# Two orders of the solved 16x16 blocks through DRAM, and no first transpose for four of the five tiles

## The reference, cut to what matters

```
a_mat = where(strict, einsum('nbhik,nbhjk->nbhij', kb, kc) * decay, 0.0)
t_inv = triangular_solve(eye + a_mat, eye, lower=True)
u = t_inv @ (vc * beta);  w = t_inv @ (kb * exp(gc))
def step(S, ...):
    v_new = u_i - w_i @ S
    o = (q_i * exp(g_i)) @ S + intra @ v_new
    S = S * exp(g_last) + (k_i * exp(g_last - g_i)).T @ v_new
```

## Time and profile before

| | us |
|---|---|
| median of the runs | 1290.6 |
| the profiled execution | 1286.11 |
| its span | 1284.3 |
| PE busy | 1144.1 (89%) |
| DVE busy | 445.2 (35%) |
| ACT busy | 329.5 (26%) |
| GpSimd (POOL) busy | 180.2 (14%) |

### The profile page before, as it was taken

One profiled execution on the slowest core, in us unless ns is written; L12 is line 12 of the kernel. 1 busy time (PEld: TensorE's weight loads), 2 busy tenths in 40 slices (PEclk: granted clock), 3 DMA queues, 4 the chain that ended last, 5 costly groups with the idle time before them and its releaser, 6 DMA issues.

```text
span 1284.3 us, 15885 instructions
## 1 busy us (share of the span) xinstructions
PE 1144.1 (89%) x6262; PEld 611.6 (48%) x6262; DVE 445.2 (35%) x843; ACT 329.5 (26%) x587; POOL 180.2 (14%) x295
## 2 busy tenths in 40 slices
PE   2699999999998987889999999999649999999990
PEld 1244456666664666888444444444333333333320
DVE  1223035877764542555420300214431111111115
ACT  4012134454453533332321000111202111111111
POOL 0000020011000257571100000000110111111100
PEclk9799999999989999899999999999959999999995
DMA  8801243343302110210231111150616999999936
GB/s 325 360 9 66 90 141 114 132 148 141 122 1 77 47 29 22 87 26 1 94 131 66 51 35 46 66 196 33 245 43 241 385 392 377 375 391 380 385 112 249
DMA packets 44063, 199.98 MB, mean 156 GB/s; under 512 B 18320, under 2 KB 23904, under 8 KB 31952
## 3 DMA queue, kind: packets, MB, share of 16 engines
q1 hardware_dynamic: 28256, 142.03, 28.8%
q10 hardware_dynamic: 4608, 30.18, 6.2%
q0 software_dynamic: 11120, 26.70, 5.8%
HBM read 190.69 MB, written 22.87 MB: 166 GB/s over the span
## 4 chain that ended last, share of the span: by engine, by line
PE 76%; DVE 9%; DMA 6%; POOL 3%; issue 3%; ACT 3%; SPq 0%; DVEq 0%; POOLq 0%; ACTq 0%
PE bank L1649 24%; PE bank L2195 11%; PE bank L1753 8%; PE bank L2216 6%; DMA arena<-h_scratch,arena 3%; PE bank L2052 3%; PE bank L2050 3%; PE bank L1802 2%; PE bank L2183 2%; PE bank L1739 2%; PE bank L1607 2%; PE bank L1908 1%; PE bank L1710 1%; DMA arena<-in_w_blocks 1%; DVE arena L1287 1%
## 5 line engine op out<-in xcount | busy, mean ns | idle before, releaser
L1649 PE MATMUL bank<-arena 128*128 128x512 f32 x720 | 315.9, 595 | 4.4 <-DVE arena L1113 3.5
L1649 PEld LDWEIGHTS bank<-arena 128*128 128x128 f32 x720 | 135.3, 190 | 169.4 <-issue 168.3
L2195 PE MATMUL bank<-arena 128*32 128x512 f32 x1536 | 172.2, 599 | 1.3 <-DVE arena L1562 1.3
L1753 PE MATMUL bank<-arena 128*128 128x320 f32 x384 | 122.0, 452 | 0.5 <-ACT arena L822 0.5
L2195 PEld LDWEIGHTS bank<-arena 128*32 128x32 f32 x1536 | 48.2, 110 | 107.8 <-issue 107.8
L2216 PE MATMUL bank<-arena 128*32 128x512 f32 x768 | 87.4, 595 | 0.8 <-ACT arena L1053 0.8
L1753 PEld LDWEIGHTS bank<-arena 128*128 128x128 f32 x384 | 68.6, 194 | 26.4 <-issue 2.1
L1575 DVE TENSOR_TENSOR arena<-arena,bank 128x256 f32<-128x256 f32 x24 | 10.1, 421 | 175.6 <-ACT arena L1047 175.6
L710 POOL DMA_INDIRECT y_scratch<-arena x24 | 24.3, 1013 | 247.8 <-DVE arena L1568 219.7
L1440 DVE TENSOR_TENSOR arena<-arena,bank 128x512 f32<-128x512 f32 x10 | 6.9, 689 | 135.8 <-PE bank L2052 135.8
L976 ACT ACTIVATE arena<-bank 128x512 f32<-128x512 f32 x20 | 11.9, 597 | 151.5 <-PE bank L1649 151.4
(11 more groups left out here) (298 smaller groups left out, 1517.4 us busy)
## 6 DMA issues: line engine op xcount, KB each, us to landing
arena<-in_w_up SPq DMA_DIRECT2D x32, 2048.0 KB, 10.1
arena<-in_w_blocks SPq DMA_DIRECT2D x27, 2048.0 KB, 7.9
arena<-in_w_down ACTq DMA_DIRECT2D x28, 1024.0 KB, 8.6
arena<-y_scratch SPq DMA_DIRECT2D x10, 512.0 KB, 7.5
arena<-in_bias POOLq DMA_DIRECT2D x3, 1536.0 KB, 11.6
arena<-in_w_down SPq DMA_DIRECT2D x4, 1024.0 KB, 8.0
arena<-in_x SPq DMA_DIRECT2D x5, 512.0 KB, 9.1
gram_scratch<-arena SPq DMA_DIRECT2D x10, 256.0 KB, 2.4
```

Of the source, the lines that this page charges most:

```text
L1649: last = mm(bank, hT[:, k, tok0[i]:tok0[i] + P], w[:, k, :], start=(k == 0), stop=(k == KC - 1))
L1753: last = mm(banks[5 + half][:, 0:HTOK], w[:, k, :], hT[:, k, half * HTOK:(half + 1) * HTOK], start=(k == 0), stop=(k == KC - 1))
L2195: last = mm(banks[2 + e % 2][at, :], rowsT[e % 2][:, k, at], eup[expert % SLOTS_W][:, k, :], start=(k == 0), stop=(k == KC - 1))
```

## The change

SP writes the solved blocks twice, once as they are and once with each 16x16 block transposed, and reads both back. For the second, GpSimd makes a transposed copy of the 64 blocks at the end of `solve`. GpSimd spreads out four matrices where it spread out two: `invT` and `inv` of both directions. For tiles 1 to 4 PE's first transposes and ACT's first copies go, and `couple(p, 1)` waits for the spread instead. Tile 0 stays as it was. The diff, cut to its core:

```diff
 def solved_out(p):
     sp.dma_start(t["solve_scratch"][p], src[0:64].rearrange("p c i -> p (c i)"))...
+    if p:
+        sp.dma_start(t["turned_scratch"][p], solve_raw[0:64].rearrange("p i c -> p (i c)")).then_inc(S["solve_io"], 16)
 def solved_back(p):
     sp.dma_start(solved_in if p else first_in, rows_of("solve_scratch"))...
+    if p:
+        sp.dma_start(turned_in, rows_of("turned_scratch")).then_inc(S["solve_back"], 16)
 def spread_out(p):
-    pool.wait_ge(S["solve_back"], 16 * p)
-    for d in range(2):
-        if d == 0 and p >= 2: pool.wait_ge(S["step_mm0"], step_at(p - 2, "vn"))
-        if d == 1 and p >= 1: pool.wait_ge(S["x_mm1"], NL * p)
-        dst = U["invT"][p % 2] if d == 0 else U["inv"]
+    pool.wait_ge(S["solve_back"], 32 * p)
+    for kind in ("invT", "inv"):
+        for d in range(2):
+            if kind == "invT" and p >= 2: pool.wait_ge(S[f"step_mm{d}"], step_at(p - 2, "vn"))
+            if kind == "inv": pool.wait_ge(S[f"x_mm{d}"], NL * p)
+            dst = U["invT"][p % 2] if kind == "invT" else U["inv"]
+            src = solved_in if (kind == "invT") == (d == 0) else turned_in
             step(pool.tensor_tensor(dst..., src..., blk..., ALU.mult), "spread")
 def solve(p, first, last):
-        step(pool.tensor_tensor(below, below, part, ALU.subtract), "solved" if n == 1 else "pool_step")
+        step(pool.tensor_tensor(below, below, part, ALU.subtract))
+    if last == SUB - 1:
+        step(pool.tensor_copy(solve_raw[0:64].rearrange("p i c -> p c i"), solve_x[0:64]), "solved")
 # ACT, per tile
-    inv_out(p, 1)
+    if p == 0: inv_out(p, 1)
 # PE
 def couple(p, n):
-        pe.wait_ge(S[f"inv{d}"], NL * p + n)
+        if p and n == 1:
+            pe.wait_ge(S["spread"], 4 * (p - 1) + 3 + d)
+            pe.wait_ge(S[f"xs{d}"], NL * p)
+        else:
+            pe.wait_ge(S[f"inv{d}"], turn_at(p, n))
...
-                if p + 1 < T:
-                    turn_inv(p + 1, 1)
```

More of the change, by code:

```diff
@@ L233, in build @@
         first_in = first_t[:, 0:2 * H_B * SUB].rearrange("p (u i) -> p u i", u=2 * H_B)
-        solved_in = solve_t[:, 0:2 * H_B * SUB].rearrange("p (u i) -> p u i", u=2 * H_B)
+        solved_in, turned_in = (solve_t[:, o:o + 2 * H_B * SUB].rearrange("p (u i) -> p u i", u=2 * H_B) for o in (0, 2 * H_B * SUB))
         assert solve_at + 2 * SUB * SUB <= KC * HALF
@@ L424, in solve_at_io, with turn_at @@
         def solve_at_io(p, k):
-            return 48 * (p - 1) + {"blocks": 32, "solved": 48}[k]
+            return 64 * (p - 1) + {"blocks": 32, "solved": 64}[k]
+        def turn_at(p, n):
+            return NL * p + n if p == 0 else NL + (NL - 1) * (p - 1) + n - 1
         def step_at(p, k):
@@ L485, in solved_back, with rows_of @@
                     sp.wait_ge(S["first_io"], 48)
-                back = bass.AP(t["solve_scratch"].tensor, p * 64 * SUB * SUB, [[SUB, P], [P * SUB, 2 * H_B], [1, SUB]])
-                sp.dma_start(solved_in if p else first_in, back).then_inc(S["solve_back" if p else "first_io"], 16)
+                def rows_of(scratch):
+                    return bass.AP(t[scratch].tensor, p * 64 * SUB * SUB, [[SUB, P], [P * SUB, 2 * H_B], [1, SUB]])
+                sp.dma_start(solved_in if p else first_in, rows_of("solve_scratch")).then_inc(S["solve_back" if p else "first_io"], 16)
+                if p:
+                    sp.dma_start(turned_in, rows_of("turned_scratch")).then_inc(S["solve_back"], 16)
             sp.dma_start(cT, t["cT"]).then_inc(S["c_in"], 16)
@@ L622, in spread_out @@
             def spread_out(p):
-                pool.wait_ge(S["solve_back"], 16 * p)
-                for d in range(2):
[L626 to L630, removed]
-                    dst = U["invT"][p % 2] if d == 0 else U["inv"]
-                    step(pool.tensor_tensor(dst.rearrange("p h (b i) -> p h b i", b=N_SUB),
-                                            solved_in[:, d * H_B:(d + 1) * H_B, :].unsqueeze(2).to_broadcast([P, H_B, N_SUB, SUB]),
-                                            blk.unsqueeze(1).unsqueeze(3).to_broadcast([P, H_B, N_SUB, SUB]), ALU.mult), "spread")
+                pool.wait_ge(S["solve_back"], 32 * p)
+                for kind in ("invT", "inv"):
+                    for d in range(2):
+                        U = unit[d]
+                        if kind == "invT" and p >= 2:
+                            pool.wait_ge(S[f"step_mm{d}"], step_at(p - 2, "vn"))
+                        if kind == "inv":
+                            pool.wait_ge(S[f"x_mm{d}"], NL * p)
+                        dst = U["invT"][p % 2] if kind == "invT" else U["inv"]
+                        src = solved_in if (kind == "invT") == (d == 0) else turned_in
+                        step(pool.tensor_tensor(dst.rearrange("p h (b i) -> p h b i", b=N_SUB),
+                                                src[:, d * H_B:(d + 1) * H_B, :].unsqueeze(2).to_broadcast([P, H_B, N_SUB, SUB]),
+                                                blk.unsqueeze(1).unsqueeze(3).to_broadcast([P, H_B, N_SUB, SUB]), ALU.mult), "spread")
             def solve(p, first, last):
@@ L920, in inv_out @@
                 for d in range(2):
[L921 to L926, removed]
+                    act.wait_ge(S[f"turn_mm{d}"], turn_at(p, n))
+                    dst = unit[d]["invT"][0] if d == 1 and n == 1 else unit[d]["inv"]
                     step(sc.activation(dst, bank4(2 * d), ACT.Copy), f"inv{d}")
@@ L941, in _ @@
             for p in range(T):
-                inv_out(p, 1)
+                if p == 0:
+                    inv_out(p, 1)
                 coupled(p, 1)
@@ L1887, in turn_inv @@
                     if n == 1:
[L1888 to L1891, removed]
+                        pe.wait_ge(S[f"prep{d}"], dprep_at(2, "gram"))
                         if d == 1:
                             src = U["inv"]
-                        if p >= 1:
-                            pe.wait_ge(S[f"xs{d}"], NL * p)
                     else:
@@ L2311 @@
     t["solve_scratch"] = nc.dram_tensor("solve_scratch", (T, 64, SUB * SUB), F32, kind="Internal").ap()
+    t["turned_scratch"] = nc.dram_tensor("turned_scratch", (T, 64, SUB * SUB), F32, kind="Internal").ap()
     t["v_scratch"] = nc.dram_tensor("v_scratch", (T - 1, P, W_A), F32, kind="Internal").ap()
```

## The result

The changed kernel took 1300.9 us (median of five, 1300.23 to 1307.58). Against the runs of the kernel before beside it the ratio is 1.0092 (95% interval 1.007 to 1.0114), 11.8 us on 1290.6, so 1302.5: half as much again as the +7.8 that I gave, and just past my upper end, 1301.8. (The two medians alone give 1.0080 or +10.3, just inside it.) The direction was right, the size was too small. A second series of the same kernel gave 1.0111 (1.0088 to 1.0135).

What follows compares the result with a forecast made beforehand. Despite PE's 89% busy share, GpSimd's chain was taken to bound the stretch at tiles 2 and 4. Delay of +6.2 at tile 4 plus 1.6 for the clock gave +7.8 us: 1290.6 to 1298.4, range 1294.3 to 1301.8.

Steps and rivals of the forecast that it cites:

- Tile 1, nothing: At tile 1 the two added spreads fit GpSimd's 2.61 us of idling, so nothing is lost; at most 2.24.
- Tile 2: At tile 2 spreads start 0.74 us late; with the added pair, masks(2, 2) and the state's DMA come 3.0 late.
- The second DMA out and back, 1.13 us beside the copy: Per tile, issuing a second DMA out (0.45) and back (0.38), plus 0.3 for slowing each other, delays the blocks.
- The interference of 0.3: Allowance of 0.3 us for the two reads back of solved blocks slowing each other.
- the bound of 1.9: Upper limit in us for that slowing, if the two reads back run one after the other; 0 if side by side.
- one of my signs of being wrong: Tile 3's couple released by PE's own order; the forecast had PE wait one us there for the third spread.
- Masks(3, 3) run on, +4.3; `q_scaled(4)` shorter: GpSimd at tile 3: masks(3, 3) no longer wait for PE, ending 4.3 us later; q_scaled(4) takes 3.1, not 3.47.
- The clock falls in front of tile 4, +1.6: PE idles 5.4 us before tile 4's couple, its clock halves, and the couple's matrix operations cost 1.6 us more.
- So nothing is given back: Behind tile 4's couple PE and DVE alternate and the next phase is bound by PE, so none of the delay is recovered.
- Rivals 3, 4 and 5: Small additions: 1292.0, chance 0.08; PE and ACT bound each tile's start: 1285.3, 0.03; waits hide the effect: 1290.6, 0.02.
- Rival 1: PE's clock does not fall before tile 4: +6.2 us, 1296.8; chance 0.17.
- Rival 2: The two reads back run one after the other at tiles 2, 3 and 4: +4.8 us, some 1303; chance 0.08.

Runs made afterwards that it cites:

- blocks_only: The kernel before, with the transposed copy and the second DMA out and back added and nobody reading them: ratio 1.0031.
- same_again: The changed kernel, unedited, run in a second series: ratio 1.0111.
- kept_busy_half: The changed kernel with identity products filling PE's idle stretches: 55 before key_key(3), 18 before tile 4's couple, 5 behind correct(p, 1): ratio 1.0082.
- spreads_only: The changed kernel without the transposed copy and second DMA out and back; all four spreads read the same blocks: ratio 1.0080.
- state_early: The kernel before, with GpSimd's two stores of the context's state issued ahead of masks(2, 1), not behind masks(2, 2): ratio 0.9952.
- inv_first: The changed kernel with the inv pair spread before the invT pair for tiles 2 to 4; couple waits for the first two: ratio 1.0067.
- change_state_early: The changed kernel with the context state's two stores issued ahead of masks(2, 1): ratio 1.0017.

## Why the prediction came out too small
By its own steps, each against the profile after:

- **Tile 1, nothing**: right, within 0.3. **The copy**: 0.60 taken, 0.62 measured (0.615 to 0.627 in its four places). The Trainium skill's rule (GPSIMD Engine Reference, Performance pitfalls for Q7 kernels), which calls strided reads dear and does not speak of writes, gave an estimated 0.40. The trace doesn't bear it out: the copy that reads in order and writes strided costs what the old one cost the other way round.
- **Tile 2**, spreads +0.74 and state store +3.0: measured 1.16 and 3.47. PE behind `key_key(3)` +2.1: 2.5, by the next product (525.95 against 523.43). Its idling before `key_key(3)`: about 14 given, 15.05 measured.
- **The second DMA out and back, 1.13 us beside the copy**: this is the step that failed on GpSimd's side. From the issue of the first DMA out to the spreads it took 4.46 (tile 3) and 4.35 (tile 4) before, and takes 6.43 and 7.15 after: 2.0 and 2.8 more. With the copy that is 2.7 and 3.5, where I had 1.8. The interference of 0.3 was too small, and the bound of 1.9 that I kept for the range would have held tile 3 and just missed tile 4. Some 1.4 of it is regular (blocks_only has 5.88 and 5.79): the second return took 2.7 to 2.8 us to land there, against 2.3 for a lone one, and its issue 0.58, not 0.38; the out DMA's issue 0.60. The rest is single long trips, at tile 4 a return of 4.0 us. They change their place: in same_again the total at tile 4 is 7.27, but there the turned blocks' DMA out took 3.3 and the return 2.9. What makes them is open.
- **What this does to tiles 3 and 4**: tile 3's spreads start 6.43 late instead of 4.8, `solve(4)` 5.8 instead of 3.9, and tile 4's spreads 9.3 instead of 5.7. Of these 3.6, 0.8 came in with the `gramT` blocks that `solve(3)` waits for. PE is at the second half of `key_key(4)` 4.9 late instead of 2.1, and tile 3's couple, for which I had one us of waiting, follows it at 557.31 without a gap, level with the end of the third spread; a couple released by PE's own order was one of my signs of being wrong. Here is the chain's part at tile 4 (start us, us, what), and the 4.67 under "issue" is the two returns, issued and in flight:
```profile
579.95 1.97 DMA turned_scratch<-arena
581.92 4.67 issue
586.61 1.07 POOL arena L643
587.76 1.07 POOL arena L643
588.91 1.08 POOL arena L643
590.04 3.67 PE bank L1917 x16
```
- **Masks(3, 3) run on, +4.3; `q_scaled(4)` shorter**: right in kind (2.79 of waiting gone, 2.95 for 3.47), but +6.35, as the spreads before them were late.
- **The clock falls in front of tile 4, +1.6**: right (4.92 us idle, 3.67 for the couple instead of 2.05, so 1.6). That the idle stretch came out near my 5.4 is luck: GpSimd came 3.6 later than I had said, and PE ended tile 3 4.2 later.
- **"So nothing is given back" and nothing more is lost behind it**: wrong. Falls behind `correct(p, 1)` in tiles 2, 3 and 4, at 532, 566 and 600, were in no term of the sum. At tiles 2 and 3 they are covered, as PE waits for GpSimd later anyway. The one at tile 4 is paid in full: from `new_values` to the couple behind it PE takes 3.27 us (600.12 to 603.39) where it took 1.78 before, 1.5 more. kept_busy_half, without both falls there, is 2.8 us shorter, most of the 3.1 that the two cost by the timelines.

So of the 5.5 that are missing, 3.6 are late spreads (9.3 against 5.7), most of them by late blocks, and 1.5 the second fall at tile 4. The rest, some 0.3, lies in small shifts behind the couple that I have not taken apart. Rivals 3, 4 and 5 are out. Rival 1 is out by the profile. Rival 2 came closest in size, but not in kind: at tile 4 the second return landed some 1.7 us after the first, yet the DMA engines were done with both by 585 (busy share 0.83, 0.55 and 0.02 in the three microseconds from 583), 1.6 us before the spreads began, so it was not the moving of one behind the other that GpSimd waited for.

## What to carry to other kernels
A small engine with 14% of the busy time can own a stage. Before work is moved onto it, follow the chain of waits through that stage and ask for each of its instructions what is queued behind it; here moving a store that stood last in its order took 6.4 us off the kernel before and 10.1 off the changed one. When a wait of a few us opens in front of TensorE, count the clock too, and also in the short gaps behind it (here 1.6 and 1.5 us at tile 4).

## What the runs showed of the hardware
- **The clock fell after idle stretches much shorter than I had compared with.** In the stretch it fell at idle stretches of 1.63, 1.85 and 2.37 us (change), 1.83 and 2.40 (spreads_only), 1.50 with 0.50 close behind it (blocks_only), and 2.63 with 1.84 close behind it (state_early). It held after 1.31 and 1.47 (before), 1.68 at tile 3 (inv_first) and 3.63. Behind the 1.80 in front of `key_key(4)` it held in the kernel before and in the change, and fell in kept_busy_half and change_state_early, where another 0.47 and 2.06 of idling followed. The length of one gap alone doesn't tell.
- **DVE and GpSimd shut each other out.** DVE's product of two SBUF operands (L1361) took 1.76 us when GpSimd's `q_scaled` had started 0.07 us before it, and 0.69 in the kernel before, when it was itself 0.02 us ahead; then GpSimd's pair took 3.49 instead of 2.95. This lengthened PE's gap at tile 2 from 1.31 to 2.37 us, behind which the clock was at 0.50. In inv_first DVE is 0.01 us ahead again, L1361 takes 0.69, and PE's gap is 1.31.
```profile
525.33 0.69 DVE L1351 TENSOR_TENSOR arena<-arena 128x512 f32<-128x512 f32 x1
525.35 3.49 POOL L611 TENSOR_TENSOR arena<-arena 128x512 f32<-128x512 f32 x2
```
```profile
527.77 2.95 POOL L620 TENSOR_TENSOR arena<-arena 128x512 f32<-128x512 f32 x2
527.84 1.76 DVE L1361 TENSOR_TENSOR arena<-arena 128x512 f32<-128x512 f32 x1
```
The first pair is the kernel before, the second the one after. The Trainium skill (SBUF — State Buffer, SBUF: two separate sides) says that the two engines share a pair of ports by an exclusive lock, also when a DVE instruction has two SBUF inputs and the GpSimd one reads SBUF, and that whoever starts first has it for the whole instruction; these rows agree.
- **A second small DMA behind the first is not free of it.** The turned blocks' return, issued 0.4 us behind the other, landed after 2.6 to 4.0 us (change) and 2.7 to 2.8 (blocks_only), against 2.3 for a lone one before. A lone one can be slow too: one of spreads_only took 3.0. Why one took 4.0 while the engines' busy share was near zero in its last microsecond and a half stays open.
